# The per-layer embedding product of a decoder block, moved from the middle of the expert loop to the tail

## What is computed

```
x = x + moe_ffn(rmsnorm(x, g_ffn), w_router, ..., w_e1, b_e1, w_e2, b_e2)     # top 4 of 32 experts
x = x + sigmoid(rmsnorm(x, g_ple) @ w_ple_gate) * (p @ w_ple)
```

## Time and profile before

| | us |
|---|---|
| median of 3 runs (lowest to highest) | 1254.29 (1253.6 to 1255.81) |
| the profiled execution | 1253.69 |
| its span, first to last instruction | 1251.6 |
| TensorE busy in it | 1147.2 (92%) |
| VectorE, ScalarE, GpSimd busy | 273.8, 188.6, 34.8 |
| mean DMA rate over the span | 358 GB/s |

### The profile page before, as it was taken

One profiled execution on the slowest core, in us unless ns is written; L12 is line 12 of the kernel. 1 busy time (PEld: TensorE's weight loads), 2 busy tenths in 40 slices (PEclk: granted clock), 3 DMA queues, 4 the chain that ended last, 5 costly groups with the idle time before them and its releaser, 6 DMA issues.

```text
span 1251.6 us, 15209 instructions
## 1 busy us (share of the span) xinstructions
PE 1147.2 (92%) x6372; PEld 477.0 (38%) x6372; DVE 273.8 (22%) x786; ACT 188.6 (15%) x405; POOL 34.8 (3%) x49
## 2 busy tenths in 40 slices
PE   7999999988999999998899888888888888888878
PEld 4455544434433334333333333333333333333334
DVE  1473534243211112111111111111111111111122
ACT  2223434222111111111110000000000000000010
POOL 2121100000000000000000000000000000000000
PEclk9999999988999999999999999999999999999999
DMA  8935050966999999999999999999999999999980
GB/s 281 321 135 187 15 135 1 398 231 261 428 426 428 429 427 428 428 429 429 424 427 428 429 428 428 428 428 429 429 430 428 428 428 427 429 429 429 427 344 34
DMA packets 51209, 448.29 MB, mean 358 GB/s; under 512 B 9265, under 2 KB 11926, under 8 KB 26502
## 3 DMA queue, kind: packets, MB, share of 16 engines
q1 hardware_dynamic: 49582, 441.45, 85.0%
q0 software_dynamic: 1264, 5.27, 1.2%
q10 hardware_dynamic: 328, 1.08, 0.3%
HBM read 446.71 MB, written 4.22 MB: 360 GB/s over the span
## 4 chain that ended last, share of the span: by engine, by line
PE 58%; DMA 38%; ACT 2%; DVE 1%; issue 0%; ACTq 0%; POOL 0%; DVEq 0%; POOLq 0%
DMA ring<-in_w_e 24%; PE ps L369 16%; DMA wbuf<-in_w_e 12%; PE ps L396 11%; PE ps L1315 7%; PE ps L1397 5%; PE ps L347 3%; PE ps L338 2%; PE ps L1514 2%; PE ps L1428 2%; PE ps L1361 2%; PE ps L1449 1%; DMA oT<-in_b_e 1%; ACT wbuf L460 1%; PE ps L386 1%; PE ps L1388 1%
## 5 line engine op out<-in xcount | busy, mean ns | idle before, releaser
L369 PE MATMUL ps<-ring,wbuf 128*64 128x512 f32 x1392 | 312.1, 595 | 35.0 <-DMA ring<-in_w_e 34.8
L369 PEld LDWEIGHTS ps<-ring,wbuf 128*64 128x64 f32 x1392 | 96.0, 136 | 238.5 <-issue 162.2
L507 DVE TENSOR_SCALAR oT<-ps 128x512 f32<-128x512 f32 x32 | 22.1, 692 | 736.2 <-PE ps L369 736.2
L369 PE MATMUL ps<-wbuf 128*64 128x512 f32 x656 | 147.8, 595 | 17.6 <-DMA wbuf<-in_w_e 17.4
L396 PE MATMUL ps<-ring,wbuf 128*64 128x512 f32 x672 | 149.5, 595 | 14.2 <-ACT wbuf L460 14.2
L456 ACT ACTIVATE oT<-oT 128x512 f32<-128x512 f32 x32 | 20.2, 630 | 509.8 <-DVE oT L507 509.8
L369 PEld LDWEIGHTS ps<-wbuf 128*64 128x64 f32 x656 | 45.2, 136 | 113.4 <-issue 75.4
L1315 PE MATMUL ps<-wbuf,hT 128*128 128x512 f32 (+2 forms) x224 | 85.4, 540 | 1.0 <-ACT hT L705 1.0
L396 PE MATMUL ps<-wbuf 128*64 128x512 f32 x352 | 78.6, 595 | 7.4 <-ACT wbuf L460 7.4
L396 PEld LDWEIGHTS ps<-ring,wbuf 128*64 128x64 f32 x672 | 46.4, 137 | 102.1 <-issue 83.9
L347 PE MATMUL ps<-wbuf 64*128 64x512 f32 x264 | 65.6, 615 | 0.7 <-ACT wbuf L462 0.7
(11 more groups left out here) (237 smaller groups left out, 763.1 us busy)
## 6 DMA issues: line engine op xcount, KB each, us to landing
ring<-in_w_e SPq DMA_DIRECT2D x129, 2048.0 KB, 38.0
wbuf<-in_w_e SPq DMA_DIRECT2D x63, 2048.0 KB, 38.0
wbuf<-in_w_in SPq DMA_DIRECT2D x9, 2048.0 KB, 8.8
wbuf<-in_w_out SPq DMA_DIRECT2D x1, 4096.0 KB, 14.2
rel_rows_repeated<-rel_rows POOLq DMA_DIRECT2D x1, 3072.0 KB, 19.6
ring<-rel_rows_repeated POOLq DMA_DIRECT2D x1, 2048.0 KB, 12.7
wbuf<-in_w_branch_a SPq DMA_DIRECT2D x2, 1024.0 KB, 9.9
wbuf<-in_w_branch_b SPq DMA_DIRECT2D x1, 2048.0 KB, 16.4
```

The lines of the kernel that those rows point to most:

```text
L369: l = mm((G, Lb)[n // 2][(n % 2) * SLOTS:(n % 2 + 1) * SLOTS, :], xeT[:, k, :], slots[at][:, r * 2 * DFF + n * 512:r * 2 * DFF + (n + 1) * ...
L507: d.tensor_scalar(gc, ps[0][:, :], LIMIT, None, ALU.min).then_inc(s["gc_ready"], 1)
```

## The change

The loads of `p` and `w_ple` move behind the last expert piece on SyncE's queue and ahead of the two halves of `w_ple_gate`; the piece numbering loses its shift. `ple_pe` and `ple_act` leave the expert loop, which becomes one loop of 32 visits on ScalarE and 3 + 27 + 2 on TensorE. In the tail TensorE transposes `p` (`ple_rows`), makes `ple(0)` and `ple(1)` ahead of `x3_rows(0,0)`, and `ple(2)` and `ple(3)` between `x3_rows(1,0)` and `gate(0)`. These use the banks 0, 1, 6, 7, so new waits keep the banks apart: for the copies of 0 and 1 ahead of the x3 transposes into them, for `x3_ready` 4 ahead of `ple(2)`, and for the copies of 2 and 3 ahead of the gate products into banks 6 and 7. VectorE waits for all four copies ahead of its products with `pl`.

```diff
-PLE_AFTER = 12
-PLE_AT = PLE_AFTER * PIECES
+PLE_AT = NE * PIECES
+PLE_BANK = [0, 1, 6, 7]
@@ expert_pe
-                with te.Fori(1, PLE_AFTER // 3) as g:
-                    three(g, 0)
-                ple_pe(te)
-                with te.Fori(PLE_AFTER // 3, NE // 3) as g:
-                    three(g, 1)
+                with te.Fori(1, NE // 3) as g:
+                    three(g)
@@ expert_act
-                with sc.Fori(0, PLE_AFTER) as it:
-                    visit(it)
-                ple_act(sc)
-                with sc.Fori(PLE_AFTER, NE) as it:
+                with sc.Fori(0, NE) as it:
                     visit(it)
@@ sync
                 for n in range(NS, NE * PIECES):
-                    if n == PLE_AT:
-                        ...
+                    sp.wait_ge(used, n - NS + 1)
                     load_first(sp, n)
+                sp.wait_ge(used, PLE_AT - NS + 1)
+                sp.dma_start(pin, ...).then_inc(ld_p, 16)
+                sp.dma_start(wple, ...).then_inc(ld_ple, 16)
@@ scalar, tail
+                def pl_copy(i):
+                    sc.wait_ge(pl_ps, i + 1)
+                    a.copy(pl[:, i // 2, (i % 2) * 512:(i % 2 + 1) * 512], ps[PLE_BANK[i]][:, :]).then_inc(pl_ev, 1)
+
+                sc.wait_ge(pt_ps, 1)
+                a.copy(pT, ps[3][:, :].rearrange("p (k t) -> p k t", k=2)).then_inc(pt_ev, 1)
+                pl_copy(0)
+                pl_copy(1)
                 for t in range(TT):
                     ...
+                pl_copy(2)
+                pl_copy(3)
@@ vector, tail
+                ve.wait_ge(pl_ev, 4)
@@ tensor, tail
                 def gate(i):
+                    if i in (2, 3):
+                        te.wait_ge(pl_ev, i + 1)
...
+                def ple_rows():
+                    te.wait_ge(ld_p, 16)
+                    ...four transposes of pin into ps[3]...
+                    te.wait_ge(pt_ev, 1)
+                    te.wait_ge(ld_ple, 16)
+
+                def ple(i):
+                    t, n = i // 2, (i % 2) * 512
+                    for k in range(2):
+                        l = mm(ps[PLE_BANK[i]][:, :], pT[:, k, t * P:(t + 1) * P], wple[:, k, n:n + 512], start=k == 0, stop=k == 1)
+                    l.then_inc(pl_ps, 1)
+
+                ple_rows()
+                ple(0)
+                ple(1)
+                te.wait_ge(pl_ev, 1)
                 x3_rows(0, 0)
+                te.wait_ge(pl_ev, 2)
                 x3_rows(0, 1)
                 x3_rows(1, 0)
+                te.wait_ge(x3_ready, 4)
+                ple(2)
+                ple(3)
                 te.wait_ge(ld_ple_gate, 32)
                 gate(0)
```

More of the change, by code:

```diff
@@ L42 @@
 PIECES = 6
-PLE_AFTER = 12
 NS = 9
-PLE_AT = PLE_AFTER * PIECES
-REST_SLOTS = [0, 1, 2, 3, 6, 7]
+PLE_AT = NE * PIECES
+REST_SLOTS = [0, 1, 2, 6, 7, 8]
 UP = 4
 RUN = 2
+PLE_BANK = [0, 1, 6, 7]
 RUN2 = 4
@@ L298, in block_kernel, with place @@
         rest = dict(s=expert_sems("b"), piece=[sem(f"piece_b{i}") for i in range(NS)], col=NE, visits=(ROUNDS - 1) * NE, pre=0)
[L300 to L308, removed]
+        def place(g, j, i):
+            at = PIECES * j + i
+            return at % NS, g * 32 + 16 * (at // NS + 1)
         def load(eng, e, i, at, signal):
@@ L317, in load_first @@
         def load_first(eng, n):
-            eng_slot = position(n) % NS
+            eng_slot = n % NS
             load(eng, n // PIECES, n % PIECES, eng_slot, piece[eng_slot])
@@ L401, in expert_pe, with three @@
                 te.wait_ge(b1_cast, 2)
-                def three(g, late, start=False):
+                def three(g, start=False):
                     for j in range(3):
-                        visit(g * 3 + j, lambda i: place(g, j, i, late), start=start and j == 0)
-                three(0, 0, True)
-                with te.Fori(1, PLE_AFTER // 3) as g:
-                    three(g, 0)
-                ple_pe(te)
-                with te.Fori(PLE_AFTER // 3, NE // 3) as g:
-                    three(g, 1)
+                        visit(g * 3 + j, lambda i: place(g, j, i), start=start and j == 0)
+                three(0, True)
+                with te.Fori(1, NE // 3) as g:
+                    three(g)
                 for j in range(NE % 3):
-                    visit(NE - NE % 3 + j, lambda i: place(NE // 3, j, i, 1))
+                    visit(NE - NE % 3 + j, lambda i: place(NE // 3, j, i))
             else:
@@ L421, in expert_pe @@
             return n_max
[L423 to L446, removed]
         def expert_act(sc, a):
@@ L577, in _ @@
                 for n in range(NS, NE * PIECES):
-                    if n == PLE_AT:
[L579 to L586, removed]
+                    sp.wait_ge(used, n - NS + 1)
                     load_first(sp, n)
+                sp.wait_ge(used, PLE_AT - NS + 1)
+                sp.dma_start(pin, io["p"][0, 0].rearrange("(t p) d -> p t d", p=P)).then_inc(ld_p, 16)
+                sp.dma_start(wple, io["w_ple"][0].rearrange("(k p) n -> p k n", p=P)).then_inc(ld_ple, 16)
                 w_gate = io["w_ple_gate"][0].rearrange("(k p) n -> p k n", p=P)
                 for i in range(2):
-                    sp.wait_ge(used, position(NE * PIECES) + i - NS)
+                    sp.wait_ge(used, PLE_AT + 1 + i - NS + 1)
                     sp.dma_start(wple_g[i], w_gate[:, 4 * i:4 * i + 4]).then_inc(ld_ple_gate, 16)
@@ L1515, in gate @@
                     l.then_inc(g_ps, 1)
+                def ple_rows():
+                    te.wait_ge(ld_p, 16)
+                    for k in range(2):
+                        for t in range(TT):
+                            l = tr(ps[3][:, k * SEQ + t * P:k * SEQ + (t + 1) * P], pin[:, t, k * P:(k + 1) * P], ident)
+                    l.then_inc(pt_ps, 1)
+                    te.wait_ge(pt_ev, 1)
+                    te.wait_ge(ld_ple, 16)
+                def ple(i):
+                    t, n = i // 2, (i % 2) * 512
+                    for k in range(2):
+                        l = mm(ps[PLE_BANK[i]][:, :], pT[:, k, t * P:(t + 1) * P], wple[:, k, n:n + 512], start=k == 0, stop=k == 1)
[4 more added lines that the diff above has]
+                te.wait_ge(pl_ev, 1)
                 x3_rows(0, 0)
+                te.wait_ge(pl_ev, 2)
                 x3_rows(0, 1)
                 x3_rows(1, 0)
+                te.wait_ge(x3_ready, 4)
+                ple(2)
+                ple(3)
                 te.wait_ge(ld_ple_gate, 32)
```

## The result

The change made the kernel slower by more than twice what was forecast: 1265.14 us median (1264.28 to 1268.06) against 1254.51 for the kernel before, ratio 1.0085 with a 95% interval of 1.0069 to 1.0101. The forecast was 1258.8, in a range of 1256.2 to 1261.6. The profiled run took 1264.46 us, its span 1262.4; up to visit 10 the two profiled runs differ by 0.23 us ((10,3) lands at 575.59 before and 575.82 after).

A forecast was written before the change was run, and what follows sets the result against it. TensorE bounds the expert stage first, the weight stream from about visit 9, and TensorE the tail. The stream's -4.73 and the tail's +9.27 sum to +4.5, giving 1258.8 us against the median of the runs; range 1256.2 to 1261.6.

The forecast's parts named there:

- The stream bounds, and the break is free: Expert stage: later visits wait 44.8 us for the weight stream, so removing TensorE's 9.32 us break after visit 11 gains nothing.
- Part 1: Expert stage: without the loads of p and w_ple, everything up to the last scatter comes 4.73 us earlier.
- The by-bytes end: Expert stage: the stream gives back only the bytes of the two loads, 1280 KB at 428 GB/s, 3.06 us.
- Part 2: End of SyncE's queue: loads of p and w_ple behind the last expert piece land before TensorE needs them; cost nothing.
- Part 3: Tail from the last scatter to gate(0): same 1.94 us gap first, gate(0) at 13.2 instead of 3.92, +9.27 us.
- the steps: Tail: gap, transposes of p, products and waits counted in TensorE's program order put gate(0) 13.18 us behind the scatter.
- the wait for x3_ready: Tail, ahead of ple(2): TensorE waits about 1 us for VectorE's add_y(3), a new wait.
- Rival 1: Tail: the granted clock falls at the new gaps, costing 1.7 us where the products run, 1260.5; chance 0.22.

The follow-up runs named there:

- all eight kernels of the table: The kernel before, the changed kernel and six variants with loads left out or added, or x3 transposes first; gaps behind the scatter were 1.67 to 4.50 us.

## Why the prediction was wrong

- **The stream bounds, and the break is free.** Right. All kernels keep 29.37 us per visit from visit 10 on, but for the visits named above, and the break left out changed nothing.
- **Part 1, the stream's gain, -4.73.** Mis-sized: -3.74. I took a distance in which something besides the loads lay. The by-bytes end, 3.06, was closer to what the loads cost (3.45), and the changed kernel then lost 1.2 us in its last visit (30.54 instead of 29.37), which no term had. The clue stood in the sum itself: 1.7 us more than the bytes, which I couldn't explain and yet took in full; p's short rows were not the reason.
- **Part 2, the moved loads cost nothing.** Right for their landing: TensorE never waited for w_ple, p or the gate halves. But the same fact, that the stream's end stays where it was (its last packet ends at 1216.6 before and 1216.9 after) while TensorE's scatter ends 3.5 us earlier, had a price that I didn't see: the branch then falls into the full stream.
- **Part 3, "ple_rows meets the same 1.94".** This is the step that failed. I had put the gap down to TensorE's own branch, with the right row beside it, and then carried its size over as if it were a constant. The runs show a load of code in it, which moved 1.1 us after ScalarE's last copy with almost no stream and 4.0 us after it against a full one. The change moved the branch by 3.5 us towards the busy part of the stream, and the gap became 4.31. Without a branch the tail has just the length that the steps give: 13.18 less the 1.94 is 11.24, and 11.2 was measured twice. The copies, the wait for x3_ready (0.94) and the order of the engines came as forecast.
- **Rival 1, the clock.** It happened, and with more force than its price: the first two products took 6.29 instead of 3.70 us, and from the first transpose of p to gate(0) it was 14.25 us against 11.28 in the changed kernel without the branch, where the clock stayed at 1.00. That is 3.0 us and not 1.7. It was given 0.22, since the gap was taken as 1.94; with the gap at 4.31 it belonged into the forecast.
- **The Trainium skill**, "Runtime: NRT & Kernel Launch", section "Instruction fetch mechanics", says that a taken branch out of what is loaded stalls until its target is fetched by a DMA. The runs without the branch agree, at 1.15 us in the kernel before and 4.3 after. I read the rule as saying whose the gap is, and passed over the word DMA.
- **The sum** over the profiled runs: forecast span 1256.1, measured 1262.4. The difference of 6.3 is made up of (31,3) landing 1.2 later than forecast (0.23 of it from ahead of visit 11), the gap 2.4, the clock 3.0, and the rest of the tail and its end 0.3 shorter.

Of the measured 0.85%, 0.34% is left when TensorE's branch is taken out of the changed kernel: the products on the path less the stream's gain. With the branch out of both kernels the tails from the scatter to gate(0) differ by 8.2 us (11.20 and 2.99). The rest of the 0.85% is the branch in the full stream and the clock that fell behind it. That the 0.34% is about what was forecast as the whole is partly luck: the forecast had 1 us too much gain from the stream, and it counted a gap behind the branch that this run does not have.

## What to carry to other kernels

A gap that the profile puts down to "issue" behind a branch is not a constant: if code has to be loaded, it shares the DMA engines with the data, so ask what the stream does at the moment when the change makes the branch happen. When a critical chain is moved earlier while the stream's end stays, a small transfer at the seam, such as an instruction load, meets the stream at its full rate. And work that is covered by a wait for the stream is free; moved into a tail that one engine bounds, it costs its full length, whatever the bytes give back.

## What the runs showed that I had not expected

- The load of code behind TensorE's branch moved 1.1 us after ScalarE's last copy with almost no stream (12 GB/s), 4.0 us after it against a full one (436 GB/s), and TensorE started 2.5 to 2.7 us behind it in all eight kernels of the table.
- The clock cost 3.0 us behind the gap of 4.31, where it lay at 0.50 for 6.8 us. Behind nearly the same gap (4.39), with the x3 transposes first, it lay there for half that time, and behind 4.50 in the kernel before with 4 MB more, also with the x3 transposes first, for 6.8 us again. So the order of the work is not shown to be what makes it cheap.
- Behind the end of a loop a visit's pieces landed 0.9 to 1.6 us late (between visits 12 and 14 in the kernels of two loops, in visit 31 in those of one); the stream was at its full rate where it was looked at (427 and 429 GB/s). Behind the second of two loops they did not. What causes it stays open.
